# First merge fed by split weights on all four projections, gates first; last down products bank by bank, last rate in two steps

## The reference, cut to what matters

```python
ya = oa @ w_proj_attn                    # 1024 x 1024
og = rmsnorm(o_fwd + o_bwd, gdn_norm_w) * silu(z)
yg = og @ w_proj_gdn                     # 1024 x 1024
merged = sigmoid(gate_a) * ya + sigmoid(gate_g) * yg   # gate_a, gate_g: h @ columns of w_in
x = x + merged @ w_out
h2 = rmsnorm(x, norm2_w)
x = x + expert_choice_ffn(h2, w_router, w_gate, w_up, w_down)   # 16 experts, 403 MB of weights
```

```python
u = square(relu(hf @ w_up_2)) @ w_down_2   # 4096 -> 1024
x = x + rms_norm(u, post_ffn_g_2)
```

## Time and profile before

| | |
|---|---|
| runs | 2880.3, 2878.84, 2876.41 us; median 2878.84 |
| the profiled execution | 2878.79 us, span 2877.0 us |
| around the span | 1.8 us |
| mean granted TensorE clock | 0.971 |
| PE busy | 2626.2 us (91%) |
| HBM read | 547.01 MB |

### The profile page before, as it was taken

One profiled execution on the slowest core, in us unless ns is written; L12 is line 12 of the kernel. 1 busy time (PEld: TensorE's weight loads), 2 busy tenths in 40 slices (PEclk: granted clock), 3 DMA queues, 4 the chain that ended last, 5 costly groups with the idle time before them and its releaser, 6 DMA issues.

```text
span 2877.0 us, 34074 instructions
## 1 busy us (share of the span) xinstructions
PE 2626.2 (91%) x14331; PEld 1711.4 (59%) x14331; DVE 982.3 (34%) x1724; ACT 723.9 (25%) x1218; POOL 605.7 (21%) x185
## 2 busy tenths in 40 slices
PE   8999979879999999888988898888889899999998
PEld 7766767777657643333323333256667766788886
DVE  3257856753121311011011110133494522360332
ACT  3257633523112110000100100033442212421212
POOL 3300644623113000000000000031121122344342
PEclk9999979979999999999999999999999999999999
DMA  4301113104225799999999999953010033333231
GB/s 162 117 16 60 61 57 118 59 2 146 84 78 204 285 406 428 428 428 428 428 428 429 428 428 429 427 208 121 30 33 16 14 112 103 110 97 101 90 101 73
DMA packets 131044, 559.36 MB, mean 194 GB/s; under 512 B 7320, under 2 KB 88672, under 8 KB 103272
## 3 DMA queue, kind: packets, MB, share of 16 engines
q1 hardware_dynamic: 130056, 551.28, 48.7%
q0 software_dynamic: 864, 6.29, 0.6%
HBM read 547.01 MB, written 10.54 MB: 194 GB/s over the span
## 4 chain that ended last, share of the span: by engine, by line
PE 71%; DMA 13%; DVE 9%; ACT 4%; issue 2%; POOL 1%; DVEq 0%; SPq 0%; ACTq 0%; POOLq 0%
DMA S<-in_w_up 11%; PE PS L612 8%; PE PS L614 8%; PE PS L613 8%; PE PS L2216 7%; PE PS L2183 7%; PE PS L602 4%; PE PS L2166 2%; PE PS L3435 2%; PE PS L3437 2%; PE PS L3438 2%; PE PS L3273 2%; PE PS L2227 1%; DMA S<-in_w_down 1%; PE PS L633 1%
## 5 line engine op out<-in xcount | busy, mean ns | idle before, releaser
L2183 PE MATMUL PS<-S 128*64 128x512 f32 x2048 | 457.1, 596 | 72.5 <-DMA S<-in_w_up 67.9
L612 PE MATMUL PS<-r_block,r_block 128*128 128x512 f32 x1040 | 419.0, 403 | 7.1 <-POOL r_block L2539 5.2
L613 PE MATMUL PS<-r_block,r_block 128*128 128x512 f32 x1040 | 405.9, 390 | 0.0
L614 PE MATMUL PS<-r_block,r_block 128*128 128x512 f32 x1008 | 393.6, 390 | 0.0
L2183 PEld LDWEIGHTS PS<-S 128*64 128x64 f32 x2048 | 140.8, 137 | 379.5 <-issue 247.1
L2539 POOL TENSOR_TENSOR r_block<-S,r_block 128x2048 fp32r<-128x2048 f32 x55 | 257.9, 4690 | 484.5 <-ACT r_block L2527 475.8
L492 POOL TENSOR_TENSOR r_block<-S,r_block 128x2048 fp32r<-128x2048 f32 x40 | 183.3, 4582 | 551.0 <-ACT r_block L484 329.4
L2216 PE MATMUL PS<-S 128*64 128x512 f32 x1024 | 225.6, 597 | 6.2 <-DMA S<-in_w_down 3.0
L612 PEld LDWEIGHTS PS<-r_block,r_block 128*128 128x128 f32 x1040 | 195.8, 188 | 56.3 <-issue 10.9
L613 PEld LDWEIGHTS PS<-r_block,r_block 128*128 128x128 f32 x1040 | 196.0, 188 | 44.9 <-issue 5.8
L2412 POOL TENSOR_TENSOR S<-S 128x1024 f32<-128x1024 f32 x4 | 9.5, 2390 | 973.5 <-DVE S L2400 973.5
(11 more groups left out here) (491 smaller groups left out, 3758.7 us busy)
## 6 DMA issues: line engine op xcount, KB each, us to landing
S<-in_w_gate SPq DMA_DIRECT2D x64, 2048.0 KB, 18.0
S<-in_w_up SPq DMA_DIRECT2D x64, 2048.0 KB, 21.0
S<-in_w_down SPq DMA_DIRECT2D x64, 2048.0 KB, 25.6
S<-in_w_in SPq DMA_DIRECT2D x57, 1024.0 KB, 5.3
S<-in_w_up SPq DMA_DIRECT2D x16, 1024.0 KB, 5.5
S<-in_w_down SPq DMA_DIRECT2D x16, 1024.0 KB, 4.9
S<-decay_rows SPq DMA_DIRECT2D x8, 1024.0 KB, 7.1
S<-in_w_out SPq DMA_DIRECT2D x8, 1024.0 KB, 5.2
```

The lines of the kernel that those rows point to most:

```text
L612: pe.matmul(out, wh, r32(HT[:, dc, :]), start=(dc == 0), stop=False)
L613: pe.matmul(out, wh, r32(low[:, dc, :]), start=False, stop=False)
L614: mm = pe.matmul(out, wl, r32(HT[:, dc, :]), start=False, stop=(dc == DC - 1))
L2183: mm = pe.matmul(PS[c * CAP:(c + 1) * CAP, 2 + 2 * m + g, :], XE[:, 2 * q + r, e * CAP:(e + 1) * CAP], w[:, r, 1024 * g + 512 * c:1024 * g ...
```

## The change

1. The two projections of the merge take the split path too. `splits` becomes the whole list of loads, and a new `split_tile_from` does the three products with high and low parts of `oa` and `og`.
2. These parts are made by new steps. `oa`: two ACT copies of 128x2048 (`attention_high_act`) in the z stage, ahead of the tanh of h = 6 and of h = 7, and two POOL subtractions (`attention_low_pool`). `og`: four ACT copies of 128x1024 (`group_high_act`) and four POOL subtractions (`group_low_pool`), each copy after two heads' `z_og`.
3. The blocks of each k come in the order 2, 3, 0, 1 (gates first), in the loads, on PE, ACT, DVE and POOL. DVE scales all four gate tiles of a k and then forms the four products.
4. `ot_back` stands before the load `("z", 3)` and `x_back` behind `("o", 1)`, the latter waiting for 32 tiles in place of 28. The first three expert loads wait for tile 30.
5. In the last down product the last two steps f are taken bank by bank: 6 matmuls for a bank, then its count.
6. The rate of the last norm is taken for the first three token blocks after the third, with an Ln on a dummy value behind its Exp, and for the fourth block after that. DVE finishes three rows, weights the fourth and finishes it.

```diff
-        splits = [n for n in where if n[0] in ("qk", "v", "g", "z", "o") or (n[0] == "m" and n[2] >= 2)]
+        splits = list(where)
+        def split_tile_from(pe, out, w, off, high, low):
+            high_w, low_w = w
+            for dc in range(DC):
+                wh, wl = (r32(v[:, dc, off:off + P]) for v in (high_w, low_w))
+                pe.matmul(out, wh, r32(high[dc]), start=(dc == 0), stop=False)
+                pe.matmul(out, wh, r32(low[:, dc, :]), start=False, stop=False)
+                mm = pe.matmul(out, wl, r32(high[dc]), start=False, stop=(dc == DC - 1))
+            return mm
@@ gate_act, in the loop over h @@
+                if h == 6:
+                    attention_high_act(act, 0)
+                    split_act(act, ("m", 0, 2))
+                if h == 7:
+                    attention_high_act(act, 1)
                 act.wait_ge(*count("z_scaled", h + 1))
...
-            split_act(act, ("m", 0, 2))
+        def attention_high_act(act, s):
+            act.wait_ge(*count("ot_back", 16))
+            act.activation(r32(half_at(M_DYN + 14336 - 2048 * s, 0)), half_at(M_DYN, s), ACT.Copy).then_inc(sem("ot_high"), 1)
+        def attention_low_pool(pool, s):
+            pool.wait_ge(*count("ot_high", s + 1))
...
+        def group_high_act(act, q):
+            act.wait_ge(*count("z_og", 2 * q + 2))
...
+        def group_low_pool(pool, q):
+            pool.wait_ge(*count("og_high", q + 1))
...
@@ merge_pe, in the loop over k @@
-                for m in range(4):
-                    (await_slot if m < 2 else await_split)(pe, ("m", k, m))
+                for m in (2, 3, 0, 1):
+                    await_split(pe, ("m", k, m))
+                    if k == 0 and m == 3:
+                        pe.wait_ge(*count("z_scaled", GH))
                     if k == 0 and m == 0:
+                        pe.wait_ge(*count("ot_low", 2))
                     if k == 0 and m == 1:
-                        pe.wait_ge(*count("z_og", GH))
+                        pe.wait_ge(*count("og_low", 4))
...
@@ merge_act, in the loop over k @@
+                for m in (2, 3, 0, 1):
+                    split_act(act, {2: ("m", k, 3), 3: ("m", k, 0), 0: ("m", k, 1)}.get(m, ("m", k + 1, 2) if k < 3 else ("o", 0)))
+                    if k == 0 and m == 2:
+                        for q in range(4):
+                            group_high_act(act, q)
+                    if m < 2:
+                        continue
...
@@ gate_pool, behind the splits of z @@
+            attention_low_pool(pool, 0)
+            split_pool(pool, ("m", 0, 2))
+            attention_low_pool(pool, 1)
+            split_pool(pool, ("m", 0, 3))
+            split_pool(pool, ("m", 0, 0))
+            for q in range(4):
+                group_low_pool(pool, q)
+            split_pool(pool, ("m", 0, 1))
+            for k in range(1, 4):
+                for m in (2, 3, 0, 1):
                     split_pool(pool, ("m", k, m))
...
@@ SP's list @@
-                if n == where[("m", 0, 0)]:
+                if n == where[("z", 3)]:
                     sp.wait_ge(*count("ot_out", 32))
                     sp.dma_start(S[:, M_DYN:M_DYN + 8 * T], ot_dram).then_inc(sem("ot_back"), 16)
...
-                if n == where[("o", 0)]:
-                    sp.wait_ge(*count("mg_proj", 28))
+                if n == where[("o", 1)]:
+                    sp.wait_ge(*count("mg_proj", 32))
                     sp.dma_start(X, a["x"][0].rearrange("(tc p) d -> p tc d", p=P)).then_inc(sem("x_back"), 16)
...
@@ ffn_pe @@
-                for f in range(FH * hf, FH * hf + FH):
+                for f in range(FH * hf, FH * hf + FH - 2 * hf):
...
+            for n in range(8):
+                for f in range(2):
...
+                mm.then_inc(sem("dn_proj"), 1)
...
@@ ffn_act, in the loop over tc behind the square @@
-            post_norm_act(act, "pn2")
+                if tc < 2:
+                    continue
+                c = slice(0, 3) if tc == 2 else slice(3, 4)
+                act.wait_ge(*count("pn2_sq", tc + 1))
+                act.activation(lnv[:, c], ss[:, c], ACT.Ln, bias=eps, scale=1.0 / D).then_inc(sem("pn2_ln"), 1)
+                act.wait_ge(*count("pn2_ln", 2 * tc - 2))
+                act.activation(rs[:, c], lnv[:, c], ACT.Exp, scale=-0.5).then_inc(sem("pn2_r"), 1)
+                if tc == 2:
+                    act.activation(warm, eps, ACT.Ln).then_inc(sem("pn2_ln"), 1)
...
@@ ffn_dve, behind the loop over the banks @@
-            weighted(2)
+            dve.wait_ge(*count("pn2_r", 1))
+            for tc in range(3):
+                finished(tc)
             weighted(3)
-            post_norm_dve(dve, "pn2", UF)
+            dve.wait_ge(*count("pn2_r", 2))
+            finished(3)
```

More of the change, by code:

```diff
@@ L430, in build_program @@
         for k in range(4):
-            for m, (w, c) in enumerate(((a["w_proj_attn"], 0), (a["w_proj_gdn"], 0),
-                                        (a["w_in"], C_GATE_A), (a["w_in"], C_GATE_G))):
-                load(("m", k, m), cols(w, c + 256 * k), "mg_proj", 8 * k + 2 * (m + 1))
+            for n, (m, w, c) in enumerate(((2, a["w_in"], C_GATE_A), (3, a["w_in"], C_GATE_G),
+                                           (0, a["w_proj_attn"], 0), (1, a["w_proj_gdn"], 0))):
+                load(("m", k, m), cols(w, c + 256 * k), "mg_proj", 8 * k + 2 * (n + 1))
         for j in range(4):
@@ L438, in slot_of @@
             n = where[name]
-            third = M_DYN + (12288 if n < where[("m", 0, 0)] else 26624)
+            third = M_DYN + (12288 if n < where[("m", 0, 2)] else 26624)
             return at(third if n % SLOTS == 2 else M_RING + (n % SLOTS) * SLOT, *((4, T) if name[0] in ("v", "o") else (DC, 256)))
@@ L1755, in gate_dve @@
             gated(GH - 1)
-        OT2 = at(M_DYN, AH, T)
+        OTL = at(M_DYN, AH, T)
+        OTH = [at(M_DYN + (14336 if h < 4 else 10240) + T * h, T) for h in range(AH)]
+        OGL = OG
+        OGH = [at(M_DYN + (23552 if h < 6 else 25600) + T * h, T) for h in range(GH)]
+        def attention_high_act(act, s):
[3 more added lines that the diff above has]
+            pool.wait_ge(*count("ot_high", s + 1))
+            o = half_at(M_DYN, s)
+            pool.tensor_tensor(r32(o), o, rounded(half_at(M_DYN + 14336 - 2048 * s, 0)), ALU.subtract).then_inc(sem("ot_low"), 1)
+        def group_high_act(act, q):
+            act.wait_ge(*count("z_og", 2 * q + 2))
+            act.activation(r32(at(M_DYN + (23552, 24576, 25600, 28672)[q], 2, T)), OG[:, 2 * q:2 * q + 2, :], ACT.Copy)\
+                .then_inc(sem("og_high"), 1)
+        def group_low_pool(pool, q):
+            pool.wait_ge(*count("og_high", q + 1))
+            o = OG[:, 2 * q:2 * q + 2, :]
+            pool.tensor_tensor(r32(o), o, rounded(at(M_DYN + (23552, 24576, 25600, 28672)[q], 2, T)), ALU.subtract)\
+                .then_inc(sem("og_low"), 1)
         MT = at(M_DYN + 4096, DC, T)
@@ L1878, in merge_dve @@
                         dve.tensor_tensor(MG_T[:, 2 * m + j, :], PS[:, 4 + 2 * m + j, :], RSB, ALU.mult).then_inc(sem("mg_scaled"), 1)
+                for m in range(2):
                     for j in range(2):
                         dve.wait_ge(*count("mg_tanh", 4 * k + 2 * m + j + 1))
+                        dve.wait_ge(*count("mg_proj", 8 * k + 4 + 2 * m + j + 1))
                         dst = MT[:, 2 * k + j, :] if m == 0 else MG_N[:, j, :]
@@ L1995, in build_program @@
         FIRST = MSLOTS + len(ONCE)
-        FREE = ((("z_og", GH), ("z_silu", GH)), (("mg_proj", 26),), (("mg_proj", 32),), (("out_proj", 12),),
+        FREE = ((("mg_proj", 30),), (("mg_proj", 30),), (("mg_proj", 30),), (("out_proj", 12),),
                 (("out_proj", 16),), (("out_proj", 16),), (("out_proj", 16),), (("out_proj", 16),), (("ro_logits", 1),))
@@ L3439, in ffn_pe @@
                                        start=False, stop=last)
-                        if f == FT - 1:
-                            mm.then_inc(sem("dn_proj"), 1)
-                    if f % 2 == 1 and f < FT - 1:
+                    if f % 2 == 1:
                         mm.then_inc(sem("dn_proj"), 1)
+            await_split2(pe, ("d", FT // 2 - 1))
+            pe.wait_ge(*count("up_lo", FT))
+            wh, wl = parts2(("d", FT // 2 - 1))
+            for n in range(8):
+                tc, s = n // 2, slice(512 * (n % 2), 512 * (n % 2) + 512)
+                for f in range(2):
+                    uh, ul = r32(U1H[:, FH - 2 + f, block_of(tc)]), r32(U1L[:, FH - 2 + f, block_of(tc)])
+                    high = r32(grid(wh.rearrange("p a b -> p (a b)"), 2)[:, f, s])
+                    pe.matmul(PS[:, n, :], uh, high, start=False, stop=False)
+                    pe.matmul(PS[:, n, :], uh, r32(wl[:, f, s]), start=False, stop=False)
+                    mm = pe.matmul(PS[:, n, :], ul, high, start=False, stop=(f == 1))
+                mm.then_inc(sem("dn_proj"), 1)
         def ffn_act(act):
@@ L3497, in weighted, with finished @@
```

(4 more changed lines are left out.)

22 lines of the change are left out of this document (10 added, 12 removed), and 16 rows, old and new, of the table CHAINS.

## The result

| | before | after |
|---|---|---|
| median of the runs | 2879.57 us (4 runs, 2876.41 to 2881.16) | 2860.66 us (4 runs, 2859.21 to 2862.73) |
| profiled execution, span | 2878.79, 2877.0 us | 2862.73, 2860.9 us |
| mean granted clock | 0.971 | 0.971 |
| PE busy | 2626.2 us | 2605.4 us |

The ratio is 0.9939, 95% interval 0.9923 to 0.9954: faster by 18.9 us by the medians and by 17.6 by the ratio, whose interval is 13 to 22 us. The forecast was 2858.5, 20.3 us less than before.

A forecast was written before the change was run, and what follows sets the result against it. PE was taken to bound the kernel, with the merge's gain carried through the transfer-bound experts. -22.8 + 2.1 + 2.4 + 1.4 - 3.4 = -20.3 from 2878.8 gave 2858.5 us; own range 2856 to 2861, 80% range 2853.5 to 2864.5.

The forecast's parts named there:

- the carry through the experts: Expert stretch behind the merge: its first load waits on an output product, so the merge's gain carries through in full.
- The rival in which the stream keeps its own clock: Experts' transfer stream doesn't start earlier, so only the tail's -3.4 us counts: 2875.4 us, chance 0.04.
- -22.8 for the matmuls: Merge on PE: 128 plain matmuls at 0.858 us become 128 split steps at 0.680, -22.8 us.
- Entry, +2.1 and +2.4: Merge entry: PE waits on POOL 2.1 us before the first gate block and 2.4 before the first delta-rule block.
- The taking of turns between DVE and POOL: Merge entry: DVE SBUF operations alternate with POOL subtractions, DVE's taking 0.5 us between two of POOL's.
- `ot_back`, +1.4: Before the merge: the load moved earlier shares DMA engines with the low parts, which PE then awaits, +1.4 us.
- the upper bound that I had for the term (3.8): The `ot_back` move costs 3.8 us if all 5.2 MB must pass before the low parts are there.
- my reading of the round robin: Low parts in POOL's own queue row would hardly feel SP's queued loads; the sum would be 1.4 us lower.
- The tail, -3.4: Kernel's end: last products bank by bank and the rate in two steps finish the rows earlier, -3.4 us.
- the rival of a held switch: Kernel's end: each of three table switches holds ACT 1.28 us longer, tail gain 0, 2861.9 us, chance 0.04.
- The rival with a heavier entry (2862.8): Merge entry: POOL's operations starve DVE, low parts behind everything, 6.4 + 3.8 us, sum -16.0, chance 0.12.
- The weights were late: Merge's steady run: loads landing in 20 us would lose 75 us, 2934 us, chance 0.03; the forecast had no wait.

The follow-up runs named there:

- the merge alone: The change without its two edits at the end (last down product and last rate as before), against the kernel before: 2865.42 us, ratio 0.9945.
- the second run: The changed kernel measured once more, nothing altered, against the kernel before: 2861.08 us, ratio 0.993.
- the best kernel: Changed kernel with `ot_back` at its old place, first gate block ahead of `oa`, group parts behind the first attention block: 2854.61 us, ratio 0.9917 to the kernel before.

## Why the prediction was right, and which term was off

The sum was -20.3, the runs gave -18.9. The time, 2860.66, lies 2.2 us above 2858.5, and that nearness is partly luck. Measured in the trace, the terms of the sum give -22.3 + 2.0 + 1.7 + 6.2 - 3.3 = -15.7, so 4.6 us less gain than forecast; one term, `ot_back`, is off by 4.8. Two small gains that the sum didn't have go the other way: about 1.2 us between the first expert load and PE's last matmul, and 0.4 behind the last row. That makes -17.3, which is within the interval of the runs; the rest to -18.9 I can place in no stretch. The load of `("z", 2)`, up to which the change does nothing, went out anywhere from 644.2 to 651.8 in the twelve traces.

**What bounds the kernel; the carry through the experts: right.** The merge's end and the first expert load moved by the same 15.1 and 15.2 us. From there to PE's last matmul the kernel after took 1956.6 us (893.61 to 2850.23), the kernel before 1953.8 (908.78 to 2862.62). That looks like 2.8 us given back, and isn't: the four other kernels with the old merge took 1957.5 to 1958.3, and the six others with the new one 1955.7 to 1957.8. The profiled execution of before was short there. By the medians of these two groups, 1957.9 and 1956.7, the kernels with the new merge are 1.2 shorter there; why is open. The rival in which the stream keeps its own clock would have left -3.4 in all and nothing for the merge alone, which gave -15.8.

**-22.8 for the matmuls: right.** With what the trace shows beside it, -22.8 + 3.5 + 2.6 + 2.0 + 1.7 = -13.0, against -12.2 measured from the load of `("z", 2)` to the merge's end. Without waits and lower clock the stretch would be 217.5 - 2.6 - 2.0 - 1.7 = 211.2, which is 22.2 to 22.3 less than the 233.4 of before: the matmuls brought 0.5 less than the term.

**Entry, +2.1 and +2.4: right**, 2.0 and 1.7 (2.1 and 1.6 in the second run). The taking of turns between DVE and POOL, read off two single cases, is what happened: the four DVE operations from 698.56 to 715.96 took 16.6 us where they take 2.9 with POOL idle, and DVE's last og ended at 717.35. The Trainium skill (SBUF — State Buffer, SBUF: two separate sides) says that the port shared by the two is locked for a whole instruction and the other engine blocks fully. The trace agrees, with these numbers.

**`ot_back`, +1.4: too small.** This is the term that was mis-sized. The first group's load had cost 2.23 us of waiting and I set 13.1 us from issue to product; here it was 664.29 - 648.91 = 15.4, and the wait of 3.5 is close to the upper bound that I had for the term (3.8). What the bounds didn't hold is what came behind it: with PE idle for 3.5 us, the clock fell and 16 products took 6.40 in place of 3.79. Together 6.2 us, 4.8 more than predicted. Alone over the kernel before, the move costs 4.3 by the runs and has only the wait.

The low parts landed in 13.4 us instead of 8.3, and the packets show how. SP's queue (q1) and POOL's (q0) of the kernel after, 654 to 660, with `ot_back` in the one and the low parts in the other (packets, MB, share):
```profile
q1 hardware_dynamic: 103, 1.69, 67.1%
q0 software_dynamic: 106, 0.87, 35.8%
```
and of the kernel before, 657 to 661, with the low parts alone:
```profile
q0 software_dynamic: 223, 1.70, 110.1%
```
The two queues moved as many packets as each other, but SP's carried 16 KB each and POOL's 8 KB: the low parts got 0.145 MB per us in place of 0.425. An estimate from these rates: `ot_back` (2.1 MB at 0.28 MB per us) takes 7.5 us, in which 1.1 MB of the low parts pass, and the other 1.0 MB take 2.4 more, 9.9 in place of 4.9 us, so 5.0 later; 5.1 were measured. By my reading of the round robin in the Trainium skill (DMA: Bandwidth & Descriptors, Queues, rings and completion order) the move would have cost nothing. The trace agrees with turns packet by packet (103 and 106) and not with my reading: I had not asked how large the packets of each queue are.

**The tail, -3.4: right.** 7.27 behind PE's end against 10.6, -3.3; alone -3.5 by the runs. The first rates were there 1.0 us behind PE's end, where the prediction had 1.2. The table loads took 1.28 each and the Exp began 0.01 us behind, so the rival of a held switch didn't show. The 1.38 for a drain that the Trainium skill (ScalarE: Activation LUTs, What ACT_TABLE_LOAD costs) gives didn't either. That both parts are needed was not said in the prediction: it took them as one.

The rival with a heavier entry (2862.8) came near the time from another side: it had POOL starving DVE, which didn't happen, and the low parts 3.8 late, where PE waited 3.5 for them. That its time lies only 2.1 us off is luck as well. The weights were late at no block of the steady run.

**What stays open**: why the clock fell behind the 3.3 to 3.5 us of waiting in the kernel after (both executions) and in the merge alone, and not in the kernel with `ot_back` alone moved (3.31 of waiting, 3.92 for the products). With `ot_back` at its old place it fell behind a wait of 2.1 at 700, and in the kernel after it didn't behind the same wait at 705; the best kernel had neither wait and no lower clock. The part of the 6.2 us that is clock, 2.6, can therefore be there or not with the same wait.

## What to carry to other kernels

Moving a load forward is not free because its data are wanted later: look at what else lands at that time, in packets of what size, and who waits for it, as 2 MB in packets of 16 KB put beside two transfers of 1 MB in packets of 8 KB cost 4 us here and won nothing. Where an engine off the critical path feeds the critical one through a short entry, list its jobs with the time at which each is wanted; with `ot_back` at its old place the same ten jobs of POOL gave 2.3, 4.9 or 1.1 us of waiting in three orders. Price an idle of PE with what the clock may do behind it, and a pair of edits at the end as a pair: one of them was worth nothing without the other.

## What the runs showed of the hardware

- DVE on two SBUF operands and POOL's subtraction don't overlap and take turns: 0.68 or 0.75 us alone, 2.4 to 4.98 beside POOL, and POOL 5.0 to 5.1 instead of 4.6. Four turns in a row went strictly one by one.
- After 3.3 to 3.5 us without work PE got a mean clock of 0.54 to 0.56 in the next 6 us (16 matmuls of 128x512 in 6.4 to 6.5 us instead of 3.8) in three executions; after 3.31 us in another kernel it kept its full clock. Behind gaps of 2.1 and 4.9 us it fell in one kernel each; behind one of 2.1 in the kernel after it didn't.
- 2 MB queued by SP beside 2 MB from POOL's queue raised the landing of the latter from 8.3 to 13.4 us. The queues shared by packets, not by bytes: 103 packets of 16 KB against 106 of 8 KB in 6 us.
